# Token halves at five norm borders, x behind the first weight slices, and another LRU order in a two-block model kernel

## The reference

```python
    for i in range(DEPTH):
        h = rmsnorm(x, norm_mix_pre[i])
        ...
        x = x + rmsnorm(m, norm_mix_post[i])
        h = rmsnorm(x, norm_ffn_pre[i])
        f = conv_ffn(h, ffn_w_up[i], ffn_conv_w[i], ffn_conv_b[i], ffn_w_down[i])
        x = x + rmsnorm(f, norm_ffn_post[i])
    return x
```

```python
    _, h = lax.associative_scan(_linear_combine, (a_t, b_t), axis=1)
    out = (h * ybr).astype(u.dtype) @ w_out + b_out
```

## Time and profile before

| | |
|---|---|
| time, median of 3 (lowest, highest) | 2927.23 us (2926.01, 2929.14) |
| the profiled execution's own time | 2929.18 us |
| its span | 2927.4 us |
| mean granted clock of PE, as a share of full speed | 0.986 |
| PE busy | 2846.5 us, 97% of the span |
| ACT, DVE, POOL busy | 1237.3, 1296.1, 1378.0 us |
| DMA moved | 256.75 MB, mean 88 GB/s |

### The profile page before, as it was taken

One profiled execution on the slowest core, in us unless ns is written; L12 is line 12 of the kernel. 1 busy time (PEld: TensorE's weight loads), 2 busy tenths in 40 slices (PEclk: granted clock), 3 DMA queues, 4 the chain that ended last, 5 costly groups with the idle time before them and its releaser, 6 DMA issues.

```text
span 2927.4 us, 33387 instructions
## 1 busy us (share of the span) xinstructions
PE 2846.5 (97%) x13263; PEld 2339.1 (80%) x13263; DVE 1296.1 (44%) x1903; ACT 1237.3 (42%) x1768; POOL 1378.0 (47%) x766
## 2 busy tenths in 40 slices
PE   9999999999999998999999999899999999999998
PEld 7777788888888787888888877778888878888887
DVE  5756516522550572653155156834313366333232
ACT  6546536422442673643244243634323346343232
POOL 5334455444445576444444548434444532344443
PEclk9999999999999999999999999899999999999999
DMA  3211122232323222223232333022233322132322
GB/s 138 86 58 51 62 91 94 94 100 94 101 94 99 72 90 89 87 94 101 94 100 95 97 97 89 8 79 89 89 105 98 97 84 69 58 101 90 105 86 87
DMA packets 88889, 256.75 MB, mean 88 GB/s; under 512 B 17440, under 2 KB 22688, under 8 KB 88736
## 3 DMA queue, kind: packets, MB, share of 16 engines
q1 hardware_dynamic: 77168, 250.57, 26.8%
q10 hardware_dynamic: 11568, 4.06, 0.6%
HBM read 248.30 MB, written 2.10 MB: 86 GB/s over the span
## 4 chain that ended last, share of the span: by engine, by line
PE 83%; DVE 7%; ACT 4%; issue 2%; DMA 2%; POOL 1%; SPq 0%; POOLq 0%; DVEq 0%; ACTq 0%
PE bank L408 23%; PE bank L410 23%; PE bank L409 23%; PE bank L436 1%; PE bank L437 1%; PE bank L441 1%; DVE bank L1318 1%; POOL wlo L2791 1%; PE bank L953 1%; PE bank L955 1%; PE bank L954 1%; ACT whi L353 1%; DVE bank L1628 1%; PE bank L2518 0%; DVE xbr L1626 0%
## 5 line engine op out<-in xcount | busy, mean ns | idle before, releaser
L2791 POOL TENSOR_TENSOR wlo<-raw,whi 128x1024 fp32r<-128x1024 f32 (+2 forms) x494 | 1129.2, 2288 | 1434.9 <-ACT whi L353 1426.6
L353 ACT ACTIVATE whi<-raw 128x1024 fp32r<-128x1024 f32 (+2 forms) x494 | 496.9, 1007 | 1083.2 <-DMA raw<-in_f_up 485.1
L408 PE MATMUL bank<-h_hi,whi 128*128 128x512 f32 x2216 | 869.0, 392 | 6.9 <-ACT xbc L1162 3.9
L410 PE MATMUL bank<-h_hi,wlo 128*128 128x512 f32 x2216 | 863.6, 390 | 0.0
L409 PE MATMUL bank<-h_lo,whi 128*128 128x512 f32 x2216 | 863.5, 390 | 0.0
L408 PEld LDWEIGHTS bank<-h_hi,whi 128*128 128x128 f32 x2216 | 416.9, 188 | 97.6 <-ACT xbc L1162 5.7
L409 PEld LDWEIGHTS bank<-h_lo,whi 128*128 128x128 f32 x2216 | 417.0, 188 | 88.2 <-issue 1.9
L410 PEld LDWEIGHTS bank<-h_hi,wlo 128*128 128x128 f32 x2216 | 416.8, 188 | 86.9
L408 PE MATMUL bank<-act_hi,whi 128*128 128x512 f32 x864 | 336.3, 389 | 0.9 <-POOL wlo L2791 0.9
L409 PE MATMUL bank<-act_lo,whi 128*128 128x512 f32 x864 | 336.1, 389 | 0.0
L410 PE MATMUL bank<-act_hi,wlo 128*128 128x512 f32 x864 | 336.1, 389 | 0.0
(11 more groups left out here) (508 smaller groups left out, 3597.5 us busy)
## 6 DMA issues: line engine op xcount, KB each, us to landing
raw<-in_f_up SPq DMA_DIRECT2D x216, 512.0 KB, 3.4
raw<-in_f_dn SPq DMA_DIRECT2D x64, 512.0 KB, 3.4
raw<-in_f_dn SPq DMA_DIRECT2D x32, 384.0 KB, 3.1
raw<-in_ssd_xbc SPq DMA_DIRECT2D x22, 512.0 KB, 3.4
raw<-in_lru_in SPq DMA_DIRECT2D x20, 512.0 KB, 3.5
raw<-in_ev_in SPq DMA_DIRECT2D x20, 512.0 KB, 3.5
raw<-in_f_dn SPq DMA_DIRECT2D x32, 320.0 KB, 2.9
raw<-in_ssd_z SPq DMA_DIRECT2D x16, 512.0 KB, 3.4
```

The lines of the kernel that those rows point to most:

```text
L353: act.activation(whi[:, s, 0:WIDTH[u]], raw[:, s, 0:WIDTH[u]], ACT.Copy).then_inc(hi_done, 1)
L408: pe.matmul(out, wh, hi, start=kt == 0, stop=False)
L410: last = pe.matmul(out, wl, hi, start=False, stop=kt == n - 1)
L2791: pool.tensor_tensor(wlo[:, s, 0:n], raw[:, s, 0:n], whi[:, s, 0:n].bitcast(F32), ALU.subtract)\
```

## The change

- **Start.** Only x's first pair stays on ACT's queue; pairs 1 to 3 go to SP's queue, each behind one set of weight slices.
- **`ssd_out`, `lru_out`.** Units 1 and 2 change places in the load order, and `pe_first` counts units as each half of the inner dimension is done. In `lru_out` PE's first two tiles wait for the high parts apart from the low parts.
- **LRU.** Scans 0 to 3 go into SBUF and stand earlier in DVE's list, roots 0 to 3 earlier in ACT's; products, scans and two of POOL's low parts take another order.
- **Token halves.** The last tile of `ssd_out`, `f0_dn1`, `lru_out`, `f1_dn1` and `f3_dn1` is computed as two halves of 256 tokens (`pe_halves`). The norm's three PE steps are cut into a step per half: `pe_base` in the middle of the first half's matmuls, `pe_part` after four blocks of the second half, `pe_spread` after nine. The work from L620 to L660 runs in sixteen steps of 256 tokens, the three tiles at once in halves too, the nine unused matmuls are gone there, and the statistic of the second norm moves into the fourth tile, with its squares from step 11 on. At the end, the sixteen scalings go by halves and the eight output DMAs carry two tiles' halves each.

The core of the diff:

```diff
+            def pe_halves(self, pe, t, rhs, stat):
+                n = sum(self.ks)
+                for e in range(2):
+                    self.pe_start(pe, self.half(e))
+                    out = self.bank(self.half(e))[:, HALF[e]]
+                    kt = 0
+                    for q, blocks in enumerate(self.ks):
+                        u = self.u0 + t * self.q + q
+                        s = u % RING
+                        w(pe, split_done, u + 1)
+                        for b in range(blocks):
+                            hi, lo = (m[:, HALF[e]] for m in rhs(kt))
+                            wh, wl = whi[:, s, b * P:b * P + P], wlo[:, s, b * P:b * P + P]
+                            pe.matmul(out, wh, hi, start=kt == 0, stop=False)
+                            pe.matmul(out, wh, lo, start=False, stop=False)
+                            last = pe.matmul(out, wl, hi, start=False, stop=kt == n - 1)
+                            kt += 1
+                            if (e, kt) == (0, n // 2):
+                                stat.pe_base(pe, 0)
+                            if (e, kt) == (1, 4):
+                                stat.pe_part(pe, 0)
+                            if (e, kt) == (1, 9):
+                                stat.pe_spread(pe, 0)
+                        if e == 1 or q == len(self.ks) - 1:
+                            last.then_inc(done, 1)
...
+                    if st.name in CROSSED:
+                        if b == st.ks[q] - 1:
+                            last.then_inc(done, 1)
+                    elif kt == n - 1:
                         last.then_inc(done, st.q)
...
+            def pe_base(self, pe, e):
                 pe.wait_ge(s_acc, 6 * self.i + 6)
-                w(pe, s_rms, self.i)
-                for c in range(NC):
-                    pe.matmul(bank[7][:, c:c + 1], chunk(nacc, c), ones[:, 0:1], start=c == 0, stop=False)
-                pe.wait_ge(s_sq, 8 * self.i + 8)
-                for c in range(NC):
-                    last = pe.matmul(bank[7][:, c:c + 1], chunk(sqb[:, 1, :], c), ones[:, 0:1], start=False, stop=c == NC - 1)
+                w(pe, s_rms, self.rms0 + e)
+                for c in (2 * e, 2 * e + 1):
+                    pe.matmul(bank[7][:, c:c + 1], chunk(nacc, c), ones[:, 0:1], start=c == 2 * e, stop=False)
+            def pe_part(self, pe, e):
+                pe.wait_ge(s_sq, self.sq0 + 8 + e)
+                for c in (2 * e, 2 * e + 1):
+                    last = pe.matmul(bank[7][:, c:c + 1], chunk(sqb[:, 1, :], c), ones[:, 0:1], start=False,
+                                     stop=c == 2 * e + 1)
                 last.then_inc(s_mm, 1)
-            def pe_spread(self, pe):
-                w(pe, s_inv, self.i)
-                pe.wait_ge(s_rec, self.n + 1)
-                for c in range(NC):
-                    last = pe.matmul(chunk(bank[6], c), rms[:, 8 + c:9 + c].broadcast_to((P, P)), ident[:], start=True, stop=True)
+            def pe_spread(self, pe, e):
+                if e == 0:
+                    w(pe, s_inv, self.inv0)
+                pe.wait_ge(s_rec, self.rec0 + e + 1)
+                for c in (2 * e, 2 * e + 1):
+                    last = pe.matmul(chunk(bank[6 + e], c), rms[:, 8 + c:9 + c].broadcast_to((P, P)), ident[:], start=True, stop=True)
                 last.then_inc(s_inv, 1)
...
+            def act(self, act, own, last, second, root):
+                self.kept0 = own.n
+                def keep(n):
+                    k, c, x = self.part(n)
+                    self.lo_ready(act, n)
+                    own(act.activation(xT[:, k, c], x, ACT.Copy))
+                def square(k):
+                    act.wait_ge(act_own, self.kept0 + KD + k + 1)
+                    self.stat.square(act, k, xT[:, k, :])
+                for n in range(2 * KD):
+                    self.post.x_ready(act, n)
+                    self.act_high(act, n)
+                    if n:
+                        keep(n - 1)
+                    if n == 1:
+                        second()
+                    if n == 3:
+                        root()
+                    if n == 7:
+                        last.split_ahead(KD * last.q - 2)
+                    if n == 11:
                         last.split_ahead(KD * last.q - 1)
-                keep(KD - 1)
+                    if n >= 11:
+                        square(n - 11)
+                keep(2 * KD - 1)
+                for k in range(5, KD):
+                    square(k)
                 self.stat.root(act, ipre[:])
...
+                self.pe_halves(pe, tiles)
+                pe.wait_ge(s_sq, self.stat.sq0 + 5)
+                st.pe_tile(pe, t, rhs_h, lambda kt: self.stat.pe(pe) if kt == 3 else None)
...
+                        if (e, kt) == (0, 1):
+                            self.post.stat.pe_base(pe, 1)
+                            self.post.stat.pe_part(pe, 1)
+                        if (e, kt) == (0, 3):
+                            self.post.stat.pe_spread(pe, 1)
...
+            add(0)
+            post.stat.inverse_columns(dve, 0)
+            post.stat.spread_ready(dve, 0)
+            for n in range(2 * KD):
+                if n == KD:
+                    post.stat.spread_ready(dve, 1)
+                if n >= 3:
+                    dve.wait_ge(act_own, pre.kept0 + n - 2)
+                post.dve_scaled(dve, n)
+                if n:
+                    pre.dve_low(dve, n - 1)
+                post.dve_sum(dve, n)
+                if n == 1:
+                    add(1)
+                if n == 3:
+                    post.stat.inverse_columns(dve, 1)
+            pre.dve_low(dve, 2 * KD - 1)
...
+            for t in range(KD - 1):
                 for q in range(st.q):
-                    if t < KD - 1 or q < st.q - 1:
-                        st.split_ahead(t * st.q + q)
-                if t == KD - 1:
-                    act.activation(rms[:, 0:1], eps[:], ACT.Sqrt)
+                    st.split_ahead(t * st.q + q)
                 st.freed(act, t)
                 stat.square(act, t, src(t))
-            stat.root_columns(act)
+            act.activation(rms[:, 0:1], eps[:], ACT.Sqrt)
+            st.freed(act, st.half(0))
+            stat.square_half(act, 0, src(KD - 1))
+            stat.root_columns(act, 0)
+            if pre is None:
+                second()
+                stat.root_columns(act, 1)
+            else:
+                pre.act(act, own, st, second, lambda: stat.root_columns(act, 1))
...
+                if name in CROSSED and k in (1, 2):
+                    n = 3 - k
...
+                sp.dma_start(xT[:, 2 * j + 2:2 * j + 4, :], dram["x"][:, 2 * j + 2:2 * j + 4, :]).then_inc(x_in[j + 1], 16)
...
-            for k in range(KD // 2):
-                act.dma_start(xT[:, 2 * k:2 * k + 2, :], dram["x"][:, 2 * k:2 * k + 2, :]).then_inc(x_in[k], 16)
+            act.dma_start(xT[:, 0:2, :], dram["x"][:, 0:2, :]).then_inc(x_in[0], 16)
```

More of the change, by code:

```diff
@@ L71 @@
 FIRST = (0, 2, 5, 8)
+CROSSED = ("ssd_out", "lru_out")
 EV_ORDER = (*range(12), *range(16, 20), *range(12, 16))
@@ L101 @@
 ]
+HALVED = ("ssd_out", "f0_dn1", "lru_out", "f1_dn1", "f3_dn1")
+HALF = slice(0, T // 2), slice(T // 2, T)
 WIDE = {"ev_in", "od_in", *(f"f{f}_up{a}" for f in range(4) for a in range(2))}
 PART0, UNIT_END, PLACE, USED = {}, [], {}, {}
-BANKS = {"ssd_dt": (3,), "ssd_z": (0, 1), "ssd_out": (4, 5, 0, 1), **{_name: range(6) for _name in WIDE}, **{f"lru_g{_g}": (4, 5, 6, 7) for _g in range(5)},
+BANKS = {"ssd_dt": (3,), "ssd_z": (0, 1), "ssd_out": (4, 5, 0, 1, 4, 5, 0, 3), **{_name: range(6) for _name in WIDE}, **{f"lru_g{_g}": (4, 5, 6, 7) for _g in range(5)},
          "uqn": (4, 5, 0, 2, 1, 3),
@@ L119 @@
         _used[_b] += 1
+        if _name in HALVED and _t == KD - 1:
+            _b = 1 if _name == "ssd_out" else 0
+            PLACE[_name, "first half"] = _b, _used[_b]
+            _used[_b] += 1
+            _n += 1
         for _ in range(_q):
@@ new lines, in __init__, with part, act_high, dve_low @@
+                Pre.count += 2 * KD if post else KD
+            def part(self, n):
+                if not self.post:
+                    return n, slice(0, T), xT[:, n, :]
+                return n % KD, HALF[n // KD], self.post.new_x(n)
+            def act_high(self, act, n):
+                k, c, x = self.part(n)
+                act.activation(h_hi[:, k, c], x, ACT.Copy, scale=self.gain(k)).then_inc(p_hi, 1)
+            def dve_low(self, dve, n):
+                k, c, x = self.part(n)
+                dve.wait_ge(p_hi, self.h0 + n + 1)
+                dve.scalar_tensor_tensor(out=h_lo[:, k, c], in0=x, scalar=self.gain(k),
+                                         in1=h_hi[:, k, c].bitcast(F32), op0=ALU.mult, op1=ALU.subtract).then_inc(p_lo, 1)
@@ L1409, in ssd_dve, with ssd_half @@
             so = stage["ssd_out"]
-            for t in range(KD):
+            for t in range(KD - 1):
                 so.tile_ready(dve, t)
```

(20 more changed lines are left out.)

327 lines of the change are left out of this document (177 added, 150 removed).

## The result

| | before | after |
|---|---|---|
| median, side by side (4 runs each) | 2926.62 us | 2982.41 us |
| ratio, 95% interval | | 1.0192 [1.0179, 1.0205] |
| span of the profiled execution | 2927.4 us | 2983.1 us |
| mean granted clock | 0.986 | 0.981 |

The change makes the kernel 56 us slower. I forecast slower, by 33, with a range that ended at 2980.0. The sign and the places are right; the size is too small by 23 us.

The account below looks back on a forecast made before the run. PE's chain of waits (83%) was taken to bound the kernel. Borders +48, start −5.5, units −1.5, LRU −8 and end 0 summed to +33 us: 2960.2 against the median 2927.23, range 2915 to 2980.

Parts of the forecast that it names:

- step 5: Fourth tile behind a border: PE waits 3.7 us for POOL's adds; tile ends at S + 35.8, not S + 26.7.
- The wait at the base: At `pe_base` inside `ssd_out`'s last tile, PE waits 5.6 us for POOL's sixth add; the four borders taken alike.
- When S comes: S is DVE's first scaling behind a border; forecast 0.3 us later at `ssd_out`, 5.3 earlier without the wait.
- The half clock: PE's clock of 0.5 behind a border's waits: 1.7 us for the first, half of that for the second.
- The sixteen steps: Three tiles behind a border: half steps of about 1.36 us, 21.8 against 17.0; tiles end at S + 25.8.
- Set to nothing, and not nothing: Behind the border, statistic and `ipre` about 3 us later; no cost set, as two more tiles run before a bank must be free.
- The gains: Outside the borders: start −5.5 us, `ssd_out`'s units −1.5, LRU −8.
- The end: Last tile and output: half steps of 0.40 us come to the same end, 0 (−2 to +2).
- each border's bound: At each border, a cost of +12 us, between +8 and +15.
- PE's pace: Rival: halves run at PE's pace, half step 1.06 us, norm hidden; about −5.5 a border, 2890 us; chance 0.15.
- no wait at the base: Rival: no wait at `pe_base` but slow half steps; a border costs +4.7 us, total 2931; chance 0.12.
- gains that fail: Rival: start transfers stay as long and LRU waits move elsewhere, both gains 0; 2973.7 us; chance 0.15.

Follow-up runs that it names:

- the run with the add sooner: Changed kernel with ACT's seventh square ahead of the last weight split and POOL's sixth add ahead of the last low part: 2958.36 us.
- the run with the sum first: Changed kernel with seventh square and POOL's sixth add earlier, POOL's second-norm adds in one go, and DVE's sum ahead of the previous step's low part: 2939.60 us.
- the two runs without halves: Kernel before with the change's other parts (x's pairs, swapped units, LRU orders) and no token halves: 2914.63 us, and 2916.43 us when run again.

## Why the forecast had the sign and not the size

The mechanism was right; what failed is the size of step 5, the fourth tile: +10 us a border forecast, +12.0 to +14.2 measured. The half clock was taken too small with it, and a late `ipre` was set to nothing.

- **The wait at the base: right.** 5.6 forecast, 5.61 measured at `ssd_out`; 24.4 us over five places. At `lru_out` it is 6.5, since the base comes after five blocks: there I had said alike.
- **When S comes: nearly right.** From DVE's copy of the seventh tile to S it was 15.83 and is 18.04 at `ssd_out`, +2.2 where I had 0.3 + 1.7; at the other borders +3.0, +3.4 and +2.3.
- **The half clock: right in kind, too small.** I had 1.7 for the first place of a border and half of it for the second, 10 in all. The 1.7 is an estimate, half of the 3.40 us at 0.50 in the earlier trace rows; no run shows this term, and what they show in its place is 1.9 to 3.1 for the first place and 3.70 − 2.05 = 1.65 for the second at `ssd_out`. It came at both places of every border, and PE worked at 0.50 for 40 us in all, not for 3.4 a time; filling the waits gave back 15 us. In the run with the add sooner, whose granted clock is 1.00 there, the base to S takes 7.75 at the first, second and fourth border; in the changed kernel 9.60, 10.81 and 9.76. So the first place cost 1.9, 3.1 and 2.0.
- **The sixteen steps: right.** The fourth tile begins at S + 25.9; I said 25.8. A step is 1.36, as forecast. As the change stands the loop decided, 1.36; in the run with the sum first, a step was DVE's own three operations, 1.25.
- **The fourth tile: this step failed.** "Two sums (0.9) and the other 15 matmuls (3.4)": I priced each sum like two matmuls of the split kind. Each sum is two records of about 0.45, so the pair takes 2.05 less 0.23 for the matmul behind it, 1.8 us; now, at half clock, with that matmul, 3.70. With the adds ending at S + 32.1 and not 31.5, the fourth tile ends at 464.87 + 14 x 0.227 = 468.05, that is S + 39.05, where I had S + 35.8 and half of 1.7. This is 2.4 us a border, 10 in all: 0.6 from the adds, 0.9 from the price of the sums, 0.8 from the whole half clock where I had half of it. (The tile's old end was read 0.4 too early: 453.22 is the start of a record of 0.79 that overlaps the sums, and the fifth tile's first matmul starts at 459.11, S + 27.1. So the difference that I should have forecast by my own terms is 9.6, and 12.0 was measured.)
- **Set to nothing, and not nothing.** "The statistic, and so `ipre`, is about 3 us later ...; so I set nothing for that." Behind the second and the fourth border a late `ipre` came out in waits. At the second, before and after:

```profile
988.82 0.63 ACT L557 ACTIVATE ipre<-rms 128x512 f32<-128x512 f32 x1
994.26 0.50 PE L408 MATMUL bank<-h_hi,whi 128*128 128x512 f32 x1 [2.03 <-DVE xbr L1600]
```

```profile
1015.01 0.63 ACT L618 ACTIVATE ipre<-rms 128x512 f32<-128x512 f32 x1
1020.44 0.50 PE L427 MATMUL bank<-h_hi,whi 128*128 128x512 f32 x1 [3.47 <-DVE xbr L1764]
```

  PE stands there ahead of the fifth tile, for a bank that DVE's convolution (L1600, now L1764) frees, and goes on 5.4 after `ipre` starts, both times. So not two more tiles but none ran before a bank had to be free, and the lateness of `ipre`, not the length of the fourth tile, made this border +17.2. At the fourth border:

```profile
1789.92 0.47 PE L427 MATMUL bank<-h_hi,whi 128*128 128x512 f32 x1 [2.23 <-POOL wlo L2971]
```

  This wait is new. Here it isn't a bank: in ACT's list DMA issues and a weight split stand behind `ipre` (the split starts 5.4 after it, before 4.6), and POOL's low part behind the split.
- **The gains: right in the time, too large in their places.** The start gave 4.6 to 4.9 (forecast 5.5), units and LRU orders 10.7 alone (forecast 9.5). In the changed kernel the stretch up to `ssd_out`'s eighth tile shows −5.2 and the LRU mixer −4.9 instead of −7 and −8. The halves didn't take this away: by the same events the two runs without halves show −5.1 and −6.7, and for the LRU mixer −5.4 and −4.5. My −8 was too much, since PE's waits around `lru_out` fell from 7.3 to 3.7 in all and not to nothing (the longest 1.5, where I had none over 1).
- **The end: nearly.** 0 forecast, +1.0. The last scalings show it, ending 2980.48, 19.0 us after DVE's copy of the seventh tile began at 2961.50; before it was 17.9, from 2906.82 to 2924.72:

```profile
2977.26 3.22 DVE L3213 SCALAR_TENSOR_TENSOR xT<-xT,cols,bank 128x256 f32<-128x256 f32 x8 [0.21 <-PE bank L640]
```

In the sum: borders and what follows from them 64.7 (62.2, 2.4 and 0.1 in the FFNs) for 48, the gains 10 for 15, the end 1 for 0. The range's upper end allowed for each border's bound, +15, or for lost gains, but not for both, and the borders came out above their bound at two places, `f0_dn1` and `lru_out`: these have the longest stretches at half clock, and the first has the wait for a bank. The three rivals fell: PE's pace (steps were 1.36), no wait at the base (5.61), and gains that fail (10 of 15 were there).

## What to carry to other kernels

A wait placed in the middle of a tile is a new price (5.61 us at `ssd_out`), even if the instruction is the same as before: look for what hid the producer, here 48 full matmuls (10.88 us) against POOL's low part and add (2.40 and 1.30), and move the producer's own neighbours first (two places in ACT's and POOL's lists gave 24 us). Before you cut a step in half, ask what bounds it: here a loop over three instructions shrank to 0.64 (from 2.13 us to 1.36) and doubled in number. When a statistic is late, look at everything that stands behind its reader in that engine's list, and at every bank that its direct users free.

## What was not expected of the hardware

The two sums with the ones matrix behind the second wait, with the matmul after them, took 3.70 us at a granted clock of 0.54 and 2.05 at 1.00: the clock added 1.65 to a wait of 4.05. Filling both waits of each border with 22 and 16 matmuls whose result is not used gave back 15 us in the whole kernel, with the waits' ends unchanged. And the length of a wait alone did not tell whether half clock follows: 1.16 us at the base, ahead of eight column sums, was followed by 3.4 us at 0.50, and 1.94 us at the statistic by none.
